# Modulation column sums folded through DRAM and taken a turn later, and row scaling made by GpSimd, in a two-network fp32 kernel

## What is computed

```python
cs = jax.nn.silu(c)
for i in range(DEPTH):                       # first network
    ada = cs @ w_ada[i] + b_ada[i]           # 1024 -> 6 * 1024
    sh1, sc1, g1, sh2, sc2, g2 = [t[:, None, :] for t in jnp.split(ada, 6, axis=-1)]
    u = x * (1.0 + sc1) + sh1
    y = _mlstm_mixer(u, ...) or _diff_attn_mixer(u, ...)
    x = _layer_norm(DEEPNORM_ALPHA * x + (1.0 + g1) * y, ln_g[i, 0], ln_b[i, 0])
    u = x * (1.0 + sc2) + sh2
    y = _conv_ffn(u, f_w_up[i], f_conv_w[i], f_conv_b[i], f_w_down[i])
    x = _layer_norm(DEEPNORM_ALPHA * x + (1.0 + g2) * y, ln_g[i, 1], ln_b[i, 1])
for i in range(DEPTH):                       # second network
    mod = (c_act @ mod_w[i] + mod_b[i])[:, None, :]
    h = modulate(rms_norm(x, norm_mix_g[i]), sh1, sc1)
    x = x + (1.0 + gt1) * y                  # y: rwkv7 or forgetting attention of h
    h = modulate(rms_norm(x, norm_mlp_g[i]), sh2, sc2)
    x = x + (1.0 + gt2) * sq_relu_mlp(h, mlp_up[i], mlp_down[i])
return rms_norm(x, final_g)
```

## Time and profile before

| | us |
|---|---|
| runs | 3153.82, 3160.3, 3168.22 |
| median | 3160.3 |
| the profiled execution | 3167.36 |
| its span | 3166.0 |
| PE busy in it | 3006.9 |
| DVE, ACT, GpSimd busy | 1982.2, 1091.1, 97.6 |
| mean granted PE clock | 0.982 of full |

### The profile page before, as it was taken

The page is one execution under the profiler, slowest core; times in us unless marked ns, Lnnn a source line. Parts: engine busy times, 40 slices in busy tenths (PEclk is TensorE's granted clock), DMA queues, the critical chain, the costliest instruction groups (busy, mean ns, idle before and its releaser), DMA issues.

```text
span 3166.0 us, 46111 instructions
## 1 busy us (share of the span) xinstructions
PE 3006.9 (95%) x19763; PEld 2441.4 (77%) x19788; DVE 1982.2 (63%) x3051; ACT 1091.1 (34%) x1667; POOL 97.6 (3%) x116
## 2 busy tenths in 40 slices
PE   6999999999988999998999999999999998899999
PEld 5877788887866888884877778778887777778887
DVE  5856897787468896787455677654444255554353
ACT  2334432233146432233333333342224344542122
POOL 0000000000000000000002222000000001000000
PEclk8999999999999999998999999999999999999999
DMA  7751554545530454542210000233322220032232
GB/s 230 192 160 54 181 179 163 183 160 173 189 105 21 157 196 146 200 163 65 95 49 11 13 13 10 103 89 104 93 93 95 83 91 27 8 107 93 94 106 80
DMA packets 236545, 346.09 MB, mean 109 GB/s; under 512 B 19621, under 2 KB 121965, under 8 KB 236341
## 3 DMA queue, kind: packets, MB, share of 16 engines
q1 hardware_dynamic: 221236, 329.63, 32.3%
q10 hardware_dynamic: 15104, 13.52, 1.4%
HBM read 340.97 MB, written 2.15 MB: 108 GB/s over the span
## 4 chain that ended last, share of the span: by engine, by line
PE 80%; DVE 11%; ACT 4%; DMA 3%; issue 1%; SPq 0%; DVEq 0%; ACTq 0%
PE bank L141 79%; DVE w_tiles L150 2%; PE bank L144 1%; DVE w_low L150 1%; DMA first_ada<-in_w_ada 1%; ACT w_high L147 1%; DMA weight_ring<-in_d_w_in 1%; DVE ada_acc L162 1%; DVE w_g L150 1%; ACT w_tiles L147 1%; DVE x_natural L162 1%; ACT stage L147 1%; ACT L147 0%; DVE x_sm L168 0%; DVE x_natural L150 0%
## 5 line engine op out<-in xcount | busy, mean ns | idle before, releaser
L150 DVE TENSOR_TENSOR w_low<-weight_ring,w_high 128x2048 fp32r<-128x2048 f32 (+2 forms) x212 | 463.7, 2187 | 455.0 <-ACT w_high L147 454.8
L147 ACT ACTIVATE w_high<-weight_ring 128x2048 fp32r<-128x2048 f32 (+2 forms) x212 | 388.1, 1831 | 610.4 <-DMA weight_ring<-in_mlp_down 179.2
L141 PE MATMUL bank<-u_high,w_high 128*128 128x512 f32 x1472 | 577.3, 392 | 12.0 <-DVE w_low L150 6.2
L141 PE MATMUL bank<-u_high,w_low 128*128 128x512 f32 x1472 | 573.8, 390 | 0.0
L141 PE MATMUL bank<-u_low,w_high 128*128 128x512 f32 x1472 | 573.8, 390 | 0.0
L141 PE MATMUL bank<-w_high,u_high 128*128 128x512 f32 x896 | 353.1, 394 | 7.2 <-DVE w_low L150 2.5
L141 PE MATMUL bank<-w_low,u_high 128*128 128x512 f32 x896 | 350.9, 392 | 0.0
L141 PE MATMUL bank<-w_high,u_low 128*128 128x512 f32 x896 | 350.6, 391 | 0.0
L141 PEld LDWEIGHTS bank<-u_high,w_high 128*128 128x128 f32 x1472 | 276.9, 188 | 70.3 <-ACT stage L147 7.0
L141 PEld LDWEIGHTS bank<-u_high,w_low 128*128 128x128 f32 x1472 | 276.9, 188 | 58.3
L141 PEld LDWEIGHTS bank<-u_low,w_high 128*128 128x128 f32 x1472 | 277.0, 188 | 56.7
(11 more groups left out here) (411 smaller groups left out, 4398.9 us busy)
## 6 DMA issues: line engine op xcount, KB each, us to landing
ada_ring<-in_mod_w SPq DMA_DIRECT2D x48, 1024.0 KB, 7.6
weight_ring<-in_f_w_up SPq DMA_DIRECT2D x44, 1024.0 KB, 5.1
ada_ring<-in_w_ada SPq DMA_DIRECT2D x40, 1024.0 KB, 7.3
weight_ring<-in_mlp_up SPq DMA_DIRECT2D x32, 1024.0 KB, 5.5
weight_ring<-in_mlp_down SPq DMA_DIRECT2D x32, 1024.0 KB, 5.0
weight_ring<-in_f_w_down SPq DMA_DIRECT2D x24, 768.0 KB, 4.6
weight_ring<-in_m_w_in SPq DMA_DIRECT2D x16, 1024.0 KB, 10.4
weight_ring<-in_d_w_in SPq DMA_DIRECT2D x12, 1024.0 KB, 5.2
```

What stands on the lines that cost most here:

```text
L141: return self.e.matmul(out, l, r, start=start, stop=stop, skip_group_check=True)
L147: return self.e.activation(out, in_, f, **kw) if self.live else QUIET
L150: return self.e.tensor_tensor(out, a, b, op) if self.live else QUIET
```

## The change

- After DVE has finished a block's ada_acc, SP stores it (256 KB) to fold_rows in DRAM and at the next turn loads it back re-arranged: 32 groups of source rows and four quarters of the columns on the 128 partitions, four pieces of 128 each. GpSimd adds the four pieces (`pool_sums`: 256 wide, then 128 wide). PE then makes one fp32 matmul of the 128x128 result with pick, a 128x4 operand that selects the quarters, at the end of the turn after the block's own, and DVE adds the bias there. DVE's first operation of the next block waits for the store to have landed, not for PE.
- The load's place is a spare 128x512 piece of m_o, d_o or r_k, or a new ada_sum_top.
- One block of m1 moves from r_out to d_out, the others by one.
- The row operations move from DVE to GpSimd (`pool_ln_rows`), in the order rows i, fold i for i below 4. They wait for the stage's transposes, as before. DVE waits for the last of them ahead of the residual.
- The f0 gate's store and load both move behind f0_up0 on ACT.

```diff
-        self.ada_bank = {}
+        self.takes, summed = {}, None
         for x in lin:
             x.first, x.turn0 = at, turn
             at += x.turns * len(x.pieces)
             turn += x.turns
-            for i, b in enumerate(x.ada or ()):
-                self.ada_bank[b] = x.group(i)
+            for i, b in enumerate(x.ada):
+                if summed is not None:
+                    self.takes[x.name, i] = summed
+                summed = b
+        self.takes["r_r", 0] = summed
...
                 if w >= AHEAD:
                     self.sp_weight(sp, w)
+                if name != "d_out" or w > L.first + i * per:
+                    self.sp_sum_in(sp)
...
             if b > len(self.ada_first):
                 sp.wait_ge(self.V, "ada used", b - 1, s)
+                if s:
+                    self.sp_sum_out(sp, b - 1)
...
+    def sp_sum_out(self, sp, b):
+        sp.wait_ge(self.V, "ada summed", b)
+        if b - 2 >= len(self.ada_first):
+            sp.wait_ge(self.fold_in, b - 2)
+        sp.dma_start(self.fold_rows[b % 2], self.aacc[:]).then_inc(*self.fold_out.landed(b))
+        self.stored_sum = b
+
+    def sp_sum_in(self, sp):
+        b = self.stored_sum
+        if b > self.loaded_sum:
+            tile, passed = self.sum_place(b)
+            sp.wait_ge(self.fold_out, b)
+            if passed:
+                sp.wait_ge(*passed)
+            if b > len(self.ada_first):
+                sp.wait_ge(self.T, "ada", b - 1)
+            src = self.fold_rows[b % 2].rearrange("a n -> (a n)").rearrange("(q p m) -> p q m", q=4, p=P)
+            sp.dma_start(tile.rearrange("p (q m) -> p q m", q=4), src).then_inc(*self.fold_in.landed(b))
+            self.loaded_sum = b
...
+    def pool_sums(self, g, *names, rows=None):
+        for name in names:
+            for i in range(self.lin[name].turns):
+                if rows and i < TT:
+                    self.pool_ln_rows(g, *rows[:3], i, rows[3])
+                if (name, i) in self.takes:
+                    b = self.takes[name, i]
+                    parts = self.sum_place(b)[0].rearrange("p (q m) -> p q m", q=4)
+                    g.wait_ge(self.fold_in, b)
+                    g.tensor_tensor(parts[:, 0:2, :], parts[:, 0:2, :], parts[:, 2:4, :], ALU.add).then_inc(*self.G.up())
+                    g.wait_ge(self.G)
+                    g.tensor_tensor(parts[:, 0, :], parts[:, 0, :], parts[:, 1, :], ALU.add).then_inc(*self.G.up("folded", b))
...
-    def pe_ada(self, pe, b):
-        bank = self.ada_bank.get(b, 7)
-        pe.wait_ge(self.V, "ada summed", b)
-        if bank in self.free:
-            pe.wait_ge(*self.free[bank])
-        for j in range(4):
-            m = pe.matmul(self.bank[bank][:, j:j + 1], self.aacc[:, j * P:(j + 1) * P], self.ones[:, 0:1], True, True)
-        m.then_inc(*self.T.up("ada", b))
-        self.free[bank] = (self.V, "mod", b)
-
-    def dve_ada_take(self, v, b):
-        _, bias, at, _ = self.ada_blocks[b]
-        v.wait_ge(self.T, "ada", b)
-        v.tensor_tensor(self.mod[:, at:at + 4], self.bank[self.ada_bank.get(b, 7)][:, 0:4], bias, ALU.add).then_inc(
-            *self.V.up("mod", b))
+    def pe_ada(self, pe, name, i):
+        if (name, i) in self.takes:
+            b, bank = self.takes[name, i], self.lin[name].group(i)
+            pe.wait_ge(self.G, "folded", b)
+            if bank in self.free:
+                pe.wait_ge(*self.free[bank])
+            pe.matmul(self.bank[bank][:, 0:4], self.sum_place(b)[0][:, 0:P], self.pick, True, True).then_inc(*self.T.up("ada", b))
+            self.free[bank] = (self.V, "mod", b)
+
+    def dve_ada_take(self, v, name, i):
+        if (name, i) in self.takes:
+            b, bank = self.takes[name, i], self.lin[name].group(i)
+            _, bias, at, _ = self.ada_blocks[b]
+            v.wait_ge(self.T, "ada", b)
+            v.tensor_tensor(self.mod[:, at:at + 4], self.bank[bank][:, 0:4], bias, ALU.add).then_inc(*self.V.up("mod", b))
...
                 if s == t == 0:
-                    v.wait_ge(self.V)
                     if b > len(self.ada_first):
-                        v.wait_ge(self.T, "ada", b - 1)
+                        v.wait_ge(self.fold_out, b - 1)
                     v.tensor_scalar(self.aacc[:], src, col, None, ALU.mult).then_inc(*self.V.up())
                 else:
...
-    def dve_ln_rows(self, v, st, tiles, n, t, turned):
+    def pool_ln_rows(self, g, st, tiles, n, t, turned):
         x = self.X[:, t, :]
-        v.wait_ge(self.T, "turned", turned, KT - 1)
-        v.wait_ge(self.ln_in[n], "rows")
-        v.wait_ge(self.V)
-        v.tensor_tensor(x, x, tiles[0][:], ALU.mult).then_inc(*self.V.up())
-        v.wait_ge(self.V)
-        v.tensor_tensor(x, x, tiles[1][:], ALU.add).then_inc(*self.V.up("rows", st, t))
+        g.wait_ge(self.T, "turned", turned, KT - 1)
+        g.wait_ge(self.ln_in[n], "rows")
+        g.tensor_tensor(x, x, tiles[0][:], ALU.mult).then_inc(*self.G.up())
+        g.wait_ge(self.G)
+        g.tensor_tensor(x, x, tiles[1][:], ALU.add).then_inc(*self.G.up("rows", st, t))
...
+        v.tensor_reduce(self.pick, self.ident.rearrange("p (r g) -> p g r", g=4), ALU.add).then_inc(*self.V.up("pick"))
...
         self.act_gate_load(a, "m", self.m_gb[:])
         self.act_norm_rows(a, self.m_ln, 0)
-        self.act_gate_store(a, "f0")
...
-        self.act_gate_load(a, st, f["gb"][:])
+        if l:
+            self.act_gate_load(a, st, f["gb"][:])
...
-        for gate in (("x",) if l else ("d",)):
-            self.act_gate_store(a, gate)
+        if l:
+            self.act_gate_store(a, "x")
+        else:
+            self.act_gate_store(a, "f0")
+            self.act_gate_load(a, "f0", f["gb"][:])
+            self.act_gate_store(a, "d")
         self.act_residual(a, st + "_dn0")
...
-        before, tiles = ("d", self.d_ln) if l else ("m", self.m_ln)
-        self.dve_ffn_up(v, l, st + "_up0", 0, lambda t: self.dve_ln_rows(v, before, tiles, 2 * l, t, st))
+        self.dve_ffn_up(v, l, st + "_up0", 0)
+        v.wait_ge(self.G, "rows", "d" if l else "m", TT - 1)
...
-        a.wait_ge(self.V, "rows", "f0", TT - 1)
+        a.wait_ge(self.G, "rows", "f0", TT - 1)
...
             self.dve_ada(v, L.ada[i])
-            self.dve_ln_rows(v, "f0", self.f[0]["ln"], 1, i, "d u")
...
+        self.pool_sums(g, "m_out")
+        self.pool_sums(g, "f0_up0", rows=("m", self.m_ln, 0, "f0"))
+        self.pool_sums(g, "f0_dn0", "f0_up1", "f0_dn1")
+        self.pool_sums(g, "d_qk", rows=("f0", self.f[0]["ln"], 1, "d u"))
+        self.pool_sums(g, "d_v")
...
+        self.pool_sums(g, "d_out")
+        self.pool_sums(g, "f1_up0", rows=("d", self.d_ln, 2, "f1"))
+        self.pool_sums(g, "f1_dn0", "f1_up1", "f1_dn1", "r_r")
```

More of the change, by code:

```diff
@@ L230, with __init__ @@
 class Net:
-    def __init__(self, nc, ctx, args, out, scratch, gate_rows):
-        self.nc, self.a, self.out, self.scratch, self.gate_rows = nc, args, out, scratch, gate_rows
+    def __init__(self, nc, ctx, args, out, scratch, gate_rows, fold_rows):
+        self.nc, self.a, self.out, self.scratch, self.gate_rows, self.fold_rows = nc, args, out, scratch, gate_rows, fold_rows
         self.T, self.V = Signal(nc, "tensor_done"), Signal(nc, "vector_done")
@@ L301, in layout @@
         self.small = take("small", [P, 96])
-        self.fold, self.eps = self.small[:, 64:80], self.small[:, 80:82]
+        self.fold, self.eps, self.pick = self.small[:, 64:80], self.small[:, 80:82], self.small[:, 88:92]
         self.X = take("x_natural", [P, TT, D])
@@ L427, in layout @@
         self.z_g = take("z_gain", [P, D])
+        ar.top = lin + 20 * 4096
+        self.sum_top = take("ada_sum_top", [P, 512])
     def gate_tiles(self, s, n, rows):
@@ L473, in linears @@
                 Linear("d_v", "t", d, 2, wide(2 * D), ada=blocks("m0", 9, 2)),
-                Linear("d_out", "t", a["d_w_out"][0], 2, wide(0), ada=blocks("m0", 11, 1))]
-        lin += [Linear("f1_up0", "f", up[1], 6, halves(0), ada=blocks("m1", 0, 6)),
+                Linear("d_out", "t", a["d_w_out"][0], 2, wide(0), ada=blocks("m0", 11, 1) + blocks("m1", 0, 1))]
+        lin += [Linear("f1_up0", "f", up[1], 6, halves(0), ada=blocks("m1", 1, 6)),
                 Linear("f1_dn0", "t", down[1], 2, wide(0), 12, 0, ada=blocks("kv", 0, 2)),
-                Linear("f1_up1", "f", up[1], 5, halves(6), ada=blocks("m1", 6, 5)),
+                Linear("f1_up1", "f", up[1], 5, halves(6), ada=blocks("m1", 7, 5)),
                 Linear("f1_dn1", "t", down[1], 2, wide(0), 10, 12 * P, ada=blocks("kv", 2, 2))]
         lin += [Linear(f"r_{n}", "t", a[f"rw_w{n}_2"][0], 2, wide(0)) for n in "rkv"]
-        lin += [Linear("r_out", "t", a["rw_wo_2"][0], 2, wide(0), ada=blocks("m1", 11, 1))]
+        lin += [Linear("r_out", "t", a["rw_wo_2"][0], 2, wide(0))]
         def mlp(layer):
@@ L515, in write @@
                 s.n = 0
-            self.free = {}
```

(29 more changed lines are left out.)

21 lines of the change are left out of this document (11 added, 10 removed).

## The result

| | median, us | range | runs |
|---|---|---|---|
| before | 3157.1 | 3153.1 to 3168.2 | 4 |
| after | 3186.7 | 3183.8 to 3188.3 | 4 |

The ratio is 1.0084 (95% interval 1.0066 to 1.0102): 0.8% slower, where 3160 was forecast. The profiled executions took 3167.4 and 3185.9. That of before lies at the slow end of its runs, so stages are compared here by their lengths in the traces, totals by the medians.

The account below looks back on a forecast made before the run. PE, busy for 95% of the span, was taken as the bound. The terms -29.0 - 12.0 + 19.6 + 9.8 + 7.0 + 4.0 = -0.6 on the median 3160.3 gave 3160 us, range 3127 to 3182.

Parts of the forecast that it names:

- column sums: End of each turn on PE: two passes of one fp32 product replace eight narrow ones, 48 x 0.605, -29.0 us.
- waits at m_o and d_v, with m_out: PE's waits for the accumulator at 228.57 and 878.96, and the lower clock behind them, both go: -12.0 us.
- stage starts: f0_up0, d_qk, f1_up0: GpSimd's rows alternate with DVE's operations of u, so PE is late 6.9, 6.2, 6.5: +19.6 us.
- turns 1 to 3: f0_up0 and f1_up0: GpSimd's rows and folds hold DVE's SBUF operations 4.4 us in two turns each: +9.8 us.
- f0's gate: f0_dn0: DVE waits 19.0 us for the gate's store and load, PE stalls 4.4, plus 2.6 for clock: +7.0 us.
- small things: 1 us of lower clock for each stage start and 1 us for 96 more transfers: +4.0 us.
- I let nothing take their place: m_o and d_v: the next weight tile's splits run before the removed waits end, so no new wait was charged against -12.0.
- GpSimd's lock: Stage starts: GpSimd and DVE wait for each other's SBUF instructions and alternate; in f0_up0 u ends at 392.2.
- priced a late start by its idle time: Stage starts: PE's lateness of 6.9, 6.2 and 6.5 us was the price, with 1 us of lower clock for each.
- GpSimd in the gaps: Rival: u's operations are not held, or for a fraction; 3125 us, half of it 3142; chance 0.24 for both.
- DVE as the bound in fourteen more turns: Rival, up stages: folds delay DVE to 23.5 us a turn, PE loses 1.4 x 14 = 20, 3180 us; chance 0.12.
- A late way through memory: Rival: sums' loads land at 25 us in nine crowded turns of m and d_qk, PE loses 36, 3196 us; chance 0.06.

Follow-up runs that it names:

- e12: The changed kernel run once more with no edit: 3183.8 us, 1.0076 of the kernel before.
- e7: Kernel before with sums a turn later from two alternating accumulators, four matmuls kept, f0's gate early, d and x gates stored later: 3147.6 us, 0.9967.
- e3: Changed kernel with the 24 row operations back on DVE, folds left on GpSimd: 3162.3 us, 1.0032 of the kernel before.
- e1: Changed kernel with the d gate's store moved from behind f0's gate load to the end of f0_dn0: 3183.2 us, 1.0084 of the kernel before.
- e6: Kernel before with only the row operations moved to GpSimd, rows 2 and 3 behind the previous turn's modulation sum: 3175.0 us, 1.0049.
- e10: Changed kernel with f0's gate stored early and each GpSimd row operation waiting for its turn's own modulation sum and fold: 3142.6 us, 0.9950 of the kernel before.
- e4: Changed kernel with GpSimd's first row operation of each stage waiting until DVE has made all of u: 3177.5 us, 1.0067 of the kernel before.

## Why the prediction was wrong, point by point

Terms as predicted, and as the turn lengths give them (a place's length less that of before, plus the 0.70 that each shorter sum saved). The terms cover the stretch from the first turn to the end of f1_dn1, with 47 of the 48 sums:

| term | predicted | measured | e12 |
|---|---|---|---|
| column sums | -29.0 | -32.9 (47 x 0.70) | -32.9 |
| waits at m_o and d_v, with m_out | -12.0 | +1.5 (m_o -1.9, m_out +3.7, d_v -0.3) | -0.6 |
| stage starts | +19.6 | +29.7 (12.1, 7.1, 10.5) | +29.0 |
| turns 1 to 3 | +9.8 | +12.8 (5.9, 6.9) | +11.0 |
| f0's gate | +7.0 | +14.9 | +7.4 |
| small things (measured: the rest) | +4.0 | +1.4 | -1.5 |
| sum | -0.6 | +27.4 | +12.4 |

Behind f1_dn1 the profiled executions differ by up to 15 us (1711 to 1727), whatever the edit, so the sum is not to be matched with the totals to a few us; the medians are 29.7 apart. (The prediction calls the profiled execution the slow one of its three runs; 3167.4 is a fourth, and nothing hangs on it.) These are the steps, the largest miss first.

- **Waits: the step "I let nothing take their place" failed**, by 13.5 us here and 11.4 in e12. The price was right: e7, which has the later sum without stores, loads and folds, gained 6.0 in m_o and 6.2 in d_v, 12.2 in all. In the changed kernel the two waits went too (the first turns are 22.0 and 22.1), but at the ends of the second turns PE idled 4.4 and 7.6 us, with half clock for 13.7 and 6.8 us from there. At m_o's end it waited for a bias addition, which stands on DVE behind a weight split, the block's eight operations on ada_acc and another split (235.3 to 246.2); ahead of them the weight tile landed 35.6 us after the start of m_o, in e7 32.8. PE reaches that end 1.4 us later in e7, with eight passes a turn. Whether that or the added transfers make the difference wasn't tried.
- **GpSimd's lock: right, and its length too.** u was to end 16.5 us behind the first matmul and ended at 386.3, 15.4 behind it (before 7.5). **The step that failed is the one that priced a late start by its idle time and allowed 1 us for the clock**, by 7.1 us over the three starts (22.6 with that allowance, 29.7 measured). Of the 12.1 lost at f0_up0, 2.3 lie ahead of the first matmul and are there with the rows on DVE too (e3). The other 9.8 lie in turn 0: 4.2 of idle time for the predicted 6.9, the rest at 1.2 GHz, which PE had for 11.5 us of this turn. In e12 turn 0 idled 4.5 and lost 7.1. The rows at hand said that such waits have a clock behind them, 6.8 and 3.4 us of it; I used them for the gate and not for the starts.
- **f0's gate: the mechanism and the 19.0 us right** (e1: idle 4.43 for 4.4; the turn 7.3 too long for 7.0), and e12 has 7.4. The 7.9 us more of the first profile came with the late landing, 8.2 us of idle time more than in e1; the term left out the d gate's store that the order showed behind the load, but that this store made the landing late isn't shown.
- **Turns 1 to 3: size right, mechanism half right.** I charged the rows with three quarters of their length since I took the PSUM operations as free; e6 shows that this is so, 3.17 us beside the rows and without them. But the rows fell on the gated unit's multiplications and casts (2.88 us instead of 0.69), which bound PE; behind the sum e10's turns were 0.7 to 1.1 above plain ones.
- **Column sums: right, and undersized.** Two passes take 0.14 us, not 0.20.
- **Rivals.** GpSimd in the gaps: false as the change stands; e10 shows a placing under which it nearly holds. DVE as the bound in fourteen more turns: false, all are at 22.01. A late way through memory: false, no wait for a fold. The time lies above the range since the waits, the starts, the gate and the turns all came out dearer than their terms, the clock having a part in each of the first three. The column sums and the small things came out 6.5 us cheaper and hid part of it.

Here the Trainium skill helps to read e6: the page "SBUF — State Buffer", section "🔬 SBUF: two separate sides", limits the lock to DVE operations in a two-port mode or with two SBUF inputs. The traces agree: a difference with two SBUF inputs took 2.60 instead of 0.69, ada_acc's accumulations, also with two, 11.96 for seven instead of 5.55 (e4), and an accumulation out of PSUM kept its 0.75 (e6). The cast of 0.43 that took 2.60 has one input; in which mode it ran no view shows. e10 makes use of this in its placing.

## What to carry to other kernels

Work moved to GpSimd cost DVE nothing beside its accumulations out of PSUM (3.17 us for four, with it and without) and cost DVE the length of GpSimd's instructions beside its operations in SBUF: 27 us lay in an order and one wait that only chose the place. A stall of PE is priced with the clock behind it; here an idle time of 4.2 to 4.5 us in a stage's first turn cost 7.1 to 9.8. When a wait is taken away, look for the next thing PE can wait for: of the 12 us that two waits were worth, the changed kernel kept next to nothing. And before a chain store, wait, load is put between two stages, know that its landing can vary; the same load took 5.6 to 13.3 us here.
